# Order of the expert kinds in a mixture-of-experts decoder step: the twelve experts of 32, 64 and 64 slots ahead of the sixteen in rounds of 32, 96, 32 and 64

## What is computed

```python
logits = x2d @ w_router + b_router
top_v, top_i = lax.top_k(logits, TOP_K)          # TOP_K = 4 of N_EXPERTS = 32
gates = jax.nn.softmax(top_v, axis=-1)
# for each expert e, on the rows (tokens) that chose it:
h = xb @ w_gate_up[e] + b_gate_up[e]             # 1024 -> 2048
out = _clamped_swiglu(h) @ w_down[e] + b_down[e] # 1024 -> 1024
y = segment_sum(out * row_w, row_tok)            # added up per token, then to x
```

## Time and profile before

| | us |
|---|---|
| median of three runs | 1100.65 (1098.61 to 1101.35) |
| the profiled execution | 1100.01 |
| its span, first to last instruction | 1098.2 |
| TensorE busy | 980.6 (89%) |
| VectorE busy | 390.8 (36%) |
| ScalarE busy | 207.5 (19%) |
| share of the weight queue (q1) of 16 DMA engines' span | 92.3% |

### The profile page before, as it was taken

How to read it: one execution, slowest core, us unless ns; L and a number is a source line. 1 busy time by engine, 2 the same in 40 slices (tenths; PEclk the granted TensorE clock), 3 DMA queues, 4 the chain that set the end, 5 groups by cost and what they waited for, 6 DMA issues and landing times.

```text
span 1098.2 us, 16660 instructions
## 1 busy us (share of the span) xinstructions
PE 980.6 (89%) x6622; PEld 416.4 (38%) x6622; DVE 390.8 (36%) x893; ACT 207.5 (19%) x451; POOL 9.6 (1%) x10
## 2 busy tenths in 40 slices
PE   9989999999997999799988999799779879869976
PEld 7777773332332333233323333233223323323322
DVE  8996565222322132213232322123333323222222
ACT  7784441110110011111101110011011111101111
POOL 2010000000000000000000000000000000000000
PEclk9989999999999999999999999899999999999999
DMA  9515947999999999999999999999999999999995
GB/s 370 139 50 191 403 202 306 408 420 428 409 426 426 428 416 427 426 428 419 427 427 427 428 423 427 428 428 429 425 427 428 426 426 428 428 427 428 428 420 233
DMA packets 43228, 425.22 MB, mean 387 GB/s; under 512 B 11412, under 2 KB 14740, under 8 KB 16656
## 3 DMA queue, kind: packets, MB, share of 16 engines
q1 hardware_dynamic: 42720, 423.56, 92.3%
q10 hardware_dynamic: 432, 0.52, 0.1%
HBM read 419.86 MB, written 2.51 MB: 385 GB/s over the span
## 4 chain that ended last, share of the span: by engine, by line
PE 61%; DMA 26%; DVE 6%; ACT 4%; issue 3%; DVEq 0%; SPq 0%; POOL 0%; ACTq 0%; POOLq 0%
PE banks L548 58%; DMA gu_ring<-w_gu_dram 26%; PE banks L998 1%; DVE raw L2025 1%; ACT s_p L1333 1%; PE banks L949 1%; ACT x_tok L1435 1%; PE banks L1075 1%; DVE hl L2037 1%; DVE hT L2042 1%; ACT s_p L1345 1%; PE banks L1005 0%; ACT gath L1446 0%; DVE s_p L1809 0%; ACT pT L1357 0%
## 5 line engine op out<-in xcount | busy, mean ns | idle before, releaser
L548 PE MATMUL banks<-gu_ring,xe 128*64 128x512 f32 x1152 | 269.6, 606 | 14.2 <-DMA gu_ring<-w_gu_dram 14.2
L2071 DVE TENSOR_TENSOR xT<-xT,banks 128x576 f32<-128x576 f32 x128 | 91.0, 751 | 534.1 <-PE banks L548 534.1
L548 PE MATMUL banks<-gu_ring,xe_s 128*32 128x512 f32 x1152 | 153.4, 624 | 48.9 <-DMA gu_ring<-w_gu_dram 30.8
L548 PEld LDWEIGHTS banks<-gu_ring,xe 128*64 128x64 f32 x1152 | 76.1, 138 | 169.3 <-issue 143.2
L548 PE MATMUL banks<-dn_ring,hT 128*64 128x512 f32 x576 | 129.3, 597 | 4.9 <-DVE hT L2042 4.9
L548 PEld LDWEIGHTS banks<-gu_ring,xe_s 128*32 128x32 f32 x1152 | 29.1, 110 | 137.5 <-issue 95.0
L548 PE MATMUL banks<-dn_ring,hT_s 128*32 128x256 f32 x1152 | 67.8, 381 | 3.3 <-ACT xe_s L1480 3.2
L548 PEld LDWEIGHTS banks<-dn_ring,hT 128*64 128x64 f32 x576 | 39.2, 137 | 79.4 <-issue 73.0
L1461 ACT ACTIVATE raw<-banks 128x512 f32<-128x512 f32 x18 | 10.8, 598 | 233.2 <-PE banks L548 233.2
L548 PE MATMUL banks<-x_tok,oh 96*64 96x512 f32 (+1 forms) x228 | 51.0, 578 | 0.5 <-DVE oh L1996 0.3
L548 PEld LDWEIGHTS banks<-dn_ring,hT_s 128*32 128x32 f32 x1152 | 34.9, 110 | 36.2 <-issue 15.1
(11 more groups left out here) (359 smaller groups left out, 850.7 us busy)
## 6 DMA issues: line engine op xcount, KB each, us to landing
gu_ring<-w_gu_dram SPq DMA_DIRECT2D x120, 2048.0 KB, 23.4
dn_ring<-w_dn_dram SPq DMA_DIRECT2D x63, 2048.0 KB, 21.2
gu_ring<-w_gu_dram SPq DMA_DIRECT2D x16, 1024.0 KB, 8.3
w_out<-w_out_dram SPq DMA_DIRECT2D x2, 2048.0 KB, 13.0
w_in<-w_in_dram SPq DMA_DIRECT2D x3, 1024.0 KB, 12.1
w_in<-w_in_dram SPq DMA_DIRECT2D x4, 512.0 KB, 8.2
w_glu<-w_glu_dram SPq DMA_DIRECT2D x1, 2048.0 KB, 8.9
dn_ring<-w_dn_dram SPq DMA_DIRECT2D x2, 1024.0 KB, 23.1
```

Of the source, the lines that this page charges most:

```text
L548: return nc.tensor.matmul(out, lhsT, rhs, start=start, stop=stop, **kw)
L2071: X.tensor_tensor(two, two, pair[(1, 3)[n % 2]].rearrange("p (h f) -> p h f", h=2)[:, :, 0:T], ALU.add).then_inc(S("acc_done"), 1)
```

## The change

The two loops change places: places 2 to 13 are now `LATE` twice, places 14 to 29 are the four rounds. Places 0, 1, 30 and 31 keep their kinds, and so each kind keeps its number of places. The loop variables and counts follow from the places. On VectorE the late experts, still written out one by one, now are places 2 to 13, with `item_order` after expert 3 and an `item_pass` after each of experts 4 to 9. SyncE's code is the same.

```diff
-FIRST_LATE = 2 + len(BODY) * ROUNDS
-KINDS = ["mid"] * 2 + list(BODY) * ROUNDS + list(LATE) * LATER + ["few"] * 2
+FIRST_BODY = 2 + len(LATE) * LATER
+KINDS = ["mid"] * 2 + list(LATE) * LATER + list(BODY) * ROUNDS + ["few"] * 2
...
         expert(1, 1, 0, KINDS[1], KINDS[0], KINDS[2], 1, 1)
+        with pe.Fori(0, LATER) as i:
+            for k in range(6):
+                p = 2 + k
+                expert(i * 6 + p, i * (WIDE[p + 6] - WIDE[p]) + WIDE[p], i * (SLIM[p + 6] - SLIM[p]) + SLIM[p],
+                       KINDS[p], KINDS[p - 1], KINDS[p + 1], k % 2, i * 3 + (p // 2 + 1))
         with pe.Fori(0, ROUNDS) as i:
             for k in range(4):
-                expert(i * 4 + (2 + k), i * (WIDE[6] - WIDE[2]) + WIDE[2 + k], i * (SLIM[6] - SLIM[2]) + SLIM[2 + k],
-                       BODY[k], BODY[k - 1], BODY[(k + 1) % 4], k % 2, i * 2 + (k // 2 + 2))
-        with pe.Fori(0, LATER) as i:
-            for k in range(6):
-                p = FIRST_LATE + k
-                expert(i * 6 + p, i * (WIDE[p + 6] - WIDE[p]) + WIDE[p], i * (SLIM[p + 6] - SLIM[p]) + SLIM[p],
-                       KINDS[p], KINDS[p - 1], KINDS[p + 1], k % 2, i * 3 + (p // 2 + 1))
+                p = FIRST_BODY + k
+                expert(i * 4 + p, i * (WIDE[p + 4] - WIDE[p]) + WIDE[p], i * (SLIM[p + 4] - SLIM[p]) + SLIM[p],
+                       BODY[k], BODY[k - 1], BODY[(k + 1) % 4], k % 2, i * 2 + (p // 2 + 1))
...
-        expert_alone(18)
-        expert_alone(19)
+        expert_alone(2)
+        expert_alone(3)
         item_order()
-        for p in range(20, 26):
+        for p in range(4, 10):
             expert_alone(p)
-            item_pass(p - 20)
+            item_pass(p - 4)
         X.tensor_copy(list_e[:, 0:ITEMS + 1], list_f[:, 0:ITEMS + 1]).then_inc(S("list_ready"), 1)
-        for p in range(26, NE - 1):
+        for p in range(10, FIRST_BODY):
             expert_alone(p)
```

More of the change, by code:

```diff
@@ L1541, in _ @@
         act_expert(1, 1, 0, KINDS[1], KINDS[0], KINDS[2])
+        with act.Fori(0, LATER) as i:
+            for k in range(6):
+                p = 2 + k
+                act_expert(i * 6 + p, i * (WIDE[p + 6] - WIDE[p]) + WIDE[p], i * (SLIM[p + 6] - SLIM[p]) + SLIM[p],
+                           KINDS[p], KINDS[p - 1], KINDS[p + 1])
         with act.Fori(0, ROUNDS) as i:
             for k in range(4):
-                act_expert(i * 4 + (2 + k), i * (WIDE[6] - WIDE[2]) + WIDE[2 + k], i * (SLIM[6] - SLIM[2]) + SLIM[2 + k],
+                p = FIRST_BODY + k
+                act_expert(i * 4 + p, i * (WIDE[p + 4] - WIDE[p]) + WIDE[p], i * (SLIM[p + 4] - SLIM[p]) + SLIM[p],
                            BODY[k], BODY[k - 1], BODY[(k + 1) % 4])
[L1546 to L1550, removed]
         act_expert(NE - 2, N_WIDE, N_SLIM - 2, "few", "mid", "few")
@@ L2165, in _ @@
         expert(1, 1, 0, KINDS[1], KINDS[0], KINDS[2], (0, 1, expert_at(0, 2)))
[L2166 to L2170, removed]
         def expert_alone(p):
             expert(p, WIDE[p], SLIM[p], KINDS[p], KINDS[p - 1], KINDS[p + 1], [expert_at(k, p - 1 + k) for k in range(3)])
-        expert_alone(18)
-        expert_alone(19)
+        expert_alone(2)
+        expert_alone(3)
         item_order()
-        for p in range(20, 26):
+        for p in range(4, 10):
             expert_alone(p)
-            item_pass(p - 20)
+            item_pass(p - 4)
         X.tensor_copy(list_e[:, 0:ITEMS + 1], list_f[:, 0:ITEMS + 1]).then_inc(S("list_ready"), 1)
-        for p in range(26, NE - 1):
+        for p in range(10, FIRST_BODY):
             expert_alone(p)
+        with dve.Fori(0, ROUNDS) as i:
+            x = [expert_at(k, i * 4 + (FIRST_BODY - 1 + k)) for k in range(6)]
+            for k in range(4):
+                p = FIRST_BODY + k
+                expert(i * 4 + p, i * (WIDE[p + 4] - WIDE[p]) + WIDE[p], i * (SLIM[p + 4] - SLIM[p]) + SLIM[p],
+                       BODY[k], BODY[k - 1], BODY[(k + 1) % 4], x[k:k + 3])
+        expert_alone(NE - 2)
         n = dve.alloc_register("dve_items")
```

## The result

The changed kernel takes 1094.09 us (median of four runs, 1093.58 to 1096.76) against 1100.78 of the kernel before beside it: a ratio of 0.9948, 95% interval 0.9927 to 0.9969. It is faster by 0.5%. The profiled execution took 1096.76, the slowest of the four; its span is 1094.9.

What follows compares the result with a forecast made beforehand. The DMA weight stream was taken as the bound. Span 1098.2 less the 2.1 us hole, other terms nothing, gave 1096.1; 1097.9 for the profiled execution, 0.6 more for the median: 1098.5 us, range 1095.2 to 1101.6.

Steps and rivals of the forecast that it cites:

- What bounds the kernel: Whole kernel: the DMA weight stream near 428 GB/s, 29.4 us an expert, is what has to be finished, not TensorE.
- B: TensorE's jumps back: their pauses were the cost, 3 x 8.4 us vanishing beneath DMA waits, giving 1075 us; chance 0.06.
- The hole, -2.1 us: Down block for expert 5, behind "many" expert 3: issued too late, it cost the stream 2.1 us, which the change removes.
- Rival 5: At that down block: the 2.1 us was a slip and no hole, so the move does nothing, 1100.6 us; chance 0.06.
- The rounds at the other end: The four rounds, now late: leads behind each "many" stay at 6 to 7 us, jumps back are covered, loss zero.
- Rivals 1 and 4: Late rounds: shrinking leads return the hole, 1100.6 us (chance 0.18); a late "few" delays each "many", 1107.5 us (0.05).
- the working without slips: Late rounds: TensorE's 118.7 against the stream's 117.6 us shrinks the lead by 1.1 a round, to 3.7 in the fourth.
- The slips: Weight landings: a 16 KB instruction packet on the slowest DMA engine costs 1.6 us; at most one more or fewer.
- Rival 2: Weight stream: one slip fewer after the change, 1098.5 - 1.6 = 1096.9 us; chance 0.14.
- The rule set aside: TensorE's instruction fetch: room for 2048 instructions would make kept loops' jumps back free; the 8.4 us jump was held against it.
- The end: After the last experts (mid, few, few): the 19.3 us from 1078.94 to the end of the span stay.
- VectorE and ScalarE: Item ordering and six passes move to experts 3 to 9: same cover, cost nothing; ScalarE only follows.

Runs made afterwards that it cites:

- e1: Kernel before, order unchanged, only TensorE's loop of the rounds started at place 0 of a 16 KB block: 1094.51 us, ratio 0.9954.
- e12: Kernel before, order unchanged, both TensorE loops started at place 0 of a block, no hint: 1095.53 us, ratio 0.9952.
- e9: Kernel before, order unchanged, both TensorE loops at place 0 with the jump-back hint: measured 2.6 us behind e5.
- e7: As e1, with 15 products on constants added after expert 1 so that TensorE is later: 1097.69 us, ratio 0.9978.
- e3: Changed kernel with both TensorE loops started at place 0 of a block: 1094.17 us, ratio 0.9948.
- e2: Changed kernel with TensorE's loop of the rounds started at place 231 of a block: 1099.25 us, ratio 0.9996 to the kernel before.
- e5: Changed kernel with TensorE's few, mid, mid loop at place 0 and a jump-back hint: 0.7% under the kernel before, about 2 us under the changed kernel.
- e6: As e1, with a quarter of expert 1's gate_up matmuls left out so that TensorE is earlier: 1093.15 us, ratio 0.9936.
- e10: Kernel before, rounds' loop kept at place 231 but given the jump-back hint: 3.6 us behind the changed order with both loops hinted.

## Why the prediction was wrong

1. **What bounds the kernel**: right. The stream runs near 428 GB/s from slice 10 on, in both, and nearly every microsecond gained is one of the stream (6.5 in the profiled pair). That B fell (e1) is the same point: pauses of TensorE ahead of the stream cost nothing.
2. **The hole, -2.1 us**: right that it goes away (issue at 271.4 with 20.9 us to landing, 437 GB/s at 281 us), wrong in its size. The term that was mis-sized rests on "a lead of 5.3 us is enough and one of 2.9 costs 2.1". The 2.1 was read from one execution; leads of 2.5 to 2.9 cost 0.3, 0.3 and 0.9 us in three others (e1, e12, e9), and in before one late DMA engine made the rest, for a cause that stays open. Rival 5, a slip and no hole, had a chance of 0.06; I put it down on the 306 GB/s, which proves nothing, since after shows 273 GB/s at 637 us with no loss. Rival 5 isn't right as it stands either: e7 shows that a late issue does make a hole. Where packets are equal, the order is worth 0.3 us (e1 and e3, e2 and before) to 1.0 (e5 and e9, less the late block; 2.6 as measured).
3. **The rounds at the other end**: right. The issues behind the four "many" lead by 5.7, 6.0, 4.8 and 5.9 us and cost nothing; forecast were 6 to 7 with none under 4. Rivals 1 and 4 did not come. With the slips gone the leads did not shrink from round to round as the working without slips had it (7.0, 5.9, 4.8, 3.7).
4. **The slips**: the mechanism was right (a 16 KB packet on the slowest engine, 1.6 us, "once per several packets"), and its count is the main step that failed: "four jumps in all. That is at most one slip more or fewer: plus or minus 1.6". I counted the jump as the unit that may fetch one block more or less. The unit is the loop: it fits or it doesn't, and if not, all its blocks come again in each iteration, nine packets a round. The change took away 26 packets of the stream (50 to 24), an eighth of which is three slips, 5 us; e1, without 27 and in the old order, measured 5.0 us less. Rival 2 had one slip.
5. **The rule set aside**: I had set the Trainium skill's room for 2048 instructions aside because the jump back cost 8.4 us each time. That showed that this loop, at this place, was fetched again; it did not show that no loop is kept. 1,663 instructions are 6.5 blocks: the question was how many blocks the loop touches before and after. The 63 packets of the earlier trace rows could have been laid out in time: nine of them stand in each round, 27 in the three rounds that repeat the first, and e1 is without just these 27. The rule's number is nearly borne out here: seven blocks stay, and eight only with the hint.
6. **The end** (19.3 us): 20.3 in the profiled execution of after, 19.3 to 21.2 in the other kernels, depending on where the last instruction blocks fall.
7. **VectorE and ScalarE**: nothing of theirs came onto the path, as forecast.

The sum in retrospect, in us: fetching -5.0, order -0.3 to -1.0, together 5.3 to 6.0 of the 6.7 between the medians; the rest is within the interval of the ratio (3.4 to 8.0 us).

What stays open: in what way a packet's cost depends on which engine is behind. e6 gained 0.9 us early and gave it back, and below 24 packets the excess hardly falls. Open too is what held one engine in before at 291.65 us, and with it the exact price of the order. Nor do I know why the sequencer keeps eight blocks only with the hint. The nine packets of each repeated round are one more than the eight blocks of the loop; a guess is that the ninth is the block behind the loop, and that eight alone would have fitted. No run tests it.

## What to carry to other kernels

In a kernel bound by DMA, count the instruction packets of a stretch and compare with the loop's size: a loop that lies in one block too many is fetched in every iteration, and each fetch delays one of the engines that carry the data, here 0.2 us of stream a packet. An edit that moves code, or a reordering, can gain or lose half a percent by that alone, so before a gain is put down to the edit, set both versions' loops to the same place in a block. A dip in the rate is a hole only if the slowest engine's transfers show it too: look whether the next block lands late. And a loss that was read from a single execution can be the dearest of several; the same lead cost 0.3 to 2.1 us here.

## What the hardware showed that I had not expected

- A TensorE loop of 1,663 instructions is fetched once when it begins at place 0 of a block (36 packets in all, e1) and in every round when it begins at place 231 (63); with a hint on the jump back, once there too (37, e10).
- One loop of 1,878 instructions is fetched again per iteration, and kept with the hint (37 and 28 packets, e3 and e5).
- A jump back to blocks that were kept has no idle time at all (806.91, 925.58); one to blocks that must be fetched has two pauses, 2.78 and 2.61 us, or 1.92 and 3.71.
- The instruction queue has a share of 0.2 to 0.4% of the span, yet in before steps of 1.55 us appear at every eighth packet, since a weight block has landed only with the last of its sixteen parts. Before the writes of `y` one such packet is free, amid them it costs about 1.6 us (e12, e9).
- A rate of 273 GB/s over 1.5 us (after, 637 us) cost the stream nothing, and one of 306 (before, 281 us) went with a loss of 2.1 us.
